# Index weights projected inside the padded rotary key matrix, and the last 16 value rows on two column strips

## The reference, cut to what matters

```python
proj = u @ w_in                 # u: 528 x 1024
qa, ka, va, qb, ckv, krope, qi, ki, wi, ga, gb = jnp.split(proj, list(np.cumsum(SPLITS)[:-1]), axis=-1)
y_a = stick_breaking(qa, ka, va, pos)                       # uses va: 528 x 512
...
krope = partial_rope(krope[:, :, None, :], pos)[:, :, 0]    # krope: 528 x 16
ki = partial_rope(ki[:, :, None, :], pos)[:, :, 0]          # ki: 528 x 64
# in dsa_attention, for each query:
s_idx = jax.nn.relu(jnp.einsum('bqhd,bkd->bqhk', qi, k_idx))
score = jnp.einsum('bqh,bqhk->bqk', wi, s_idx)              # wi: 528 x 8, one index weight per head
_, sel = lax.top_k(score, topk)
```

## Time and profile before

| | |
|---|---|
| median of 3 runs | 2608.38 us (2603.45 to 2608.44) |
| the profiled execution | 2611.73 us |
| its span in the profile | 2609.8 us |
| TensorE busy, share of the span | 2296.4 us, 88% |
| VectorE busy | 961.0 us, 37% |
| ScalarE busy | 451.7 us, 17% |
| mean granted clock of TensorE | 0.94 |
| DMA over the span | 137 GB/s |

### The profile page before, as it was taken

How to read it: one execution, slowest core, us unless ns; L and a number is a source line. 1 busy time by engine, 2 the same in 40 slices (tenths; PEclk the granted TensorE clock), 3 DMA queues, 4 the chain that set the end, 5 groups by cost and what they waited for, 6 DMA issues and landing times.

```text
span 2609.8 us, 26212 instructions
## 1 busy us (share of the span) xinstructions
PE 2296.4 (88%) x10107; PEld 1560.8 (60%) x10107; DVE 961.0 (37%) x1961; ACT 451.7 (17%) x851; POOL 50.8 (2%) x76
## 2 busy tenths in 40 slices
PE   7999999989989999999989997779999587777783
PEld 5888887336644888887558774456785332222231
DVE  5454433133743455434310207876651300000003
ACT  2000001253351001000210014432113000000001
POOL 0000000000000000000000000000000000000001
PEclk9999999999999999999989987789999699989997
DMA  3232222111005323231132210000332589999996
GB/s 128 65 97 87 87 88 91 46 35 33 1 9 181 118 79 97 75 119 57 41 90 69 65 41 1 1 9 1 97 113 92 226 372 429 428 430 429 429 415 246
DMA packets 172359, 359.92 MB, mean 138 GB/s; under 512 B 15665, under 2 KB 144305, under 8 KB 155874
## 3 DMA queue, kind: packets, MB, share of 16 engines
q1 hardware_dynamic: 163744, 326.89, 33.8%
q0 software_dynamic: 5600, 21.10, 2.1%
q10 hardware_dynamic: 2914, 10.56, 1.0%
HBM read 337.49 MB, written 21.04 MB: 137 GB/s over the span
## 4 chain that ended last, share of the span: by engine, by line
PE 27%; DMA 12%; DVE 5%; issue 4%; DVEq 2%; ACT 1%; POOLq 1%; SPq 1%; POOL 0%; ACTq 0%
DMA M<-w 12%; PE PS L2905 7%; PE PS L69 6%; PE PS L2289 5%; PE PS L2471 2%; PE PS L1563 1%; DVE M L1880 1%; DVEq L1884 1%; PE PS L2044 1%; DVE M L1874 1%; PE PS L1573 1%; PE PS L1986 0%; POOLq L258 0%; DVE M L1896 0%; PE PS L1800 0%
## 5 line engine op out<-in xcount | busy, mean ns | idle before, releaser
L575 PE MATMUL PS<-M 128*128 128x256 f32 x2464 | 542.4, 382 | 12.5 <-DVE M L324 7.3
L575 PEld LDWEIGHTS PS<-M 128*128 128x128 f32 x2464 | 469.2, 191 | 86.6 <-DMA M<-w_ffn_up 13.2
L2905 PE MATMUL PS<-M 128*64 128x512 f32 x1536 | 370.3, 640 | 97.4 <-DMA M<-w 93.1
L2905 PEld LDWEIGHTS PS<-M 128*64 128x64 f32 x1536 | 122.6, 147 | 333.6 <-issue 279.6
L606 PE MATMUL PS<-M 128*128 128x256 f32 x1232 | 268.6, 379 | 4.8 <-DVE M L690 2.5
L606 PEld LDWEIGHTS PS<-M 128*128 128x128 f32 x1232 | 233.4, 190 | 41.7 <-issue 10.3
L69 PE MATMUL PS<-M 128*128 128x264 f32 (+1 forms) x824 | 208.5, 416 | 23.0 <-ACT M L313 9.6
L69 PEld LDWEIGHTS PS<-M 128*128 128x128 f32 x824 | 160.0, 196 | 71.0 <-issue 23.2
L2975 DVE TENSOR_TENSOR M<-M,PS 128x512 f32<-128x512 f32 x16 | 11.0, 687 | 434.3 <-PE PS L2905 434.3
L693 DVE TENSOR_TENSOR M<-M,PS 128x256 f32<-128x256 f32 x220 | 92.6, 421 | 201.1 <-PE PS L575 197.0
L2289 PE MATMUL PS<-M 128*128 128x264 f32 x616 | 142.8, 394 | 8.1 <-DVE M L2388 5.1
(11 more groups left out here) (365 smaller groups left out, 2263.5 us busy)
## 6 DMA issues: line engine op xcount, KB each, us to landing
M<-w SPq DMA_DIRECT2D x64, 2048.0 KB, 21.2
M<-w SPq DMA_DIRECT2D x64, 1024.0 KB, 21.9
M<-w_ffn_gate SPq DMA_DIRECT2D x22, 1024.0 KB, 5.4
M<-w_ffn_up SPq DMA_DIRECT2D x22, 1024.0 KB, 5.4
M<-w_ffn_down SPq DMA_DIRECT2D x16, 1024.0 KB, 5.1
M<-w_in SPq DMA_DIRECT2D x13, 1024.0 KB, 5.3
M<-w_in SPq DMA_DIRECT2D x25, 512.0 KB, 3.8
expert_rows<-M POOLq DMA_DIRECT2D x2, 4096.0 KB, 24.4
```

What stands on the lines that cost most here:

```text
L575: last = nc.tensor.matmul(PS[:, 3 * half + BANK[p], 0:HALF], lhs[:, a, :], rhs[:, a, :], start=p in FIRST and a == 0, stop=p in LAST and a ...
L2905: last = nc.tensor.matmul(PS[ROWS * k:ROWS * k + ROWS, bank, :], wide[:, a * P + ROWS * k:a * P + ROWS * k + ROWS], weights(k), start=star ...
```

## The change

`wi` is no longer a product of its own. Its 8 weight columns are loaded into columns 32 to 39 of KRW, which were zero, so the product that makes the rotary key leaves the index weights, turned, on partitions 32 to 39 of its PSUM banks. ACT copies these 8 rows to a new tile WIT, and the rows 0 to 31 and 64 to 127 to R1; rows 32 to 63 of R1 are set to zero by POOL. Five small jobs then turn WIT back: WIT is stationary (8 partitions, 128 tokens) and an 8 by 8 corner of the identity moves. The last job makes the last 32 tokens on four strips, as before.

The 16-token jobs of `va` are split: columns 0 to 127 of the chunk go to partitions 0 to 15 of the bank, columns 128 to 255 to partitions 32 to 47, in alternate products. ACT copies them out with two instructions.

```diff
-        WIW, WUK, WUV = at(SCR + 6240, KD, 8), at(SCR + 6304, 4 * P), at(SCR + 6816, S1)
+        WUK, WUV = at(SCR + 6304, 4 * P), at(SCR + 6816, S1)
+        WIT = at(SCR + 7536, S2)[0:8]
...
-            sp.dma_start(WIW, w2cols(OFF["wi"], 8)).then_inc(small_in, 16)
+            sp.dma_start(KRW[:, :, 32:40], w2cols(OFF["wi"], 8)).then_inc(small_in, 16)
...
         def proj2_pool(pool):
+            pool.wait_ge(r_out, 2 + 7)
+            nc.gpsimd.memset(R1[32:64, 0, :], 0.0).then_inc(tails_set, 1)
             pool.wait_ge(ck_out, 1)
...
+                    strips = 1 if w == P else 2
                     for a in range(KD):
-                        last = nc.tensor.matmul(PS[0:w, 2 + (k - 1) % 2, 0:256], xnT[:, a, lo:lo + w],
-                                                slot(s, 0, KD, 256)[:, a, :], start=a == 0, stop=a == KD - 1)
+                        for m in range(strips):
+                            cols = slice(m * P, m * P + 256 // strips)
+                            last = nc.tensor.matmul(PS[32 * m:32 * m + w, 2 + (k - 1) % 2, 0:256 // strips],
+                                                    xnT[:, a, lo:lo + w], slot(s, 0, KD, 256)[:, a, cols],
+                                                    start=a == 0, stop=a == KD - 1)
...
             for t in range(5):
                 k = after("pe", v2_free)
                 pe.wait_ge(v2_free, k)
+                if t == 0:
+                    pe.wait_ge(ck_out, 1)
                 for m in range(4 if t == 4 else 1):
                     to, lo, w = (slice(32 * m, 32 * m + 32), TAIL0, 32) if t == 4 else (slice(0, P), t * P, P)
-                    for a in range(KD):
-                        last = nc.tensor.matmul(PS[to, 2 + (k - 1) % 2, 0:8], xnT[:, a, lo:lo + w], WIW[:, a, :],
-                                                start=a == 0, stop=a == KD - 1)
+                    last = nc.tensor.matmul(PS[to, 2 + (k - 1) % 2, 0:8], WIT[:, lo:lo + w], ident[0:8, 0:8], start=True, stop=True)
                 last.then_inc(v2_ready, 1)
-            pe.wait_ge(tails_set, 1)
+            pe.wait_ge(tails_set, 2)
...
-            for k in range(2):
-                act.wait_ge(ck_ready, k + 1)
-                nc.scalar.activation(G2.row(R1[:, k, :]), G2.psum(PS, 2 * k), ACT.Copy).then_inc(r_x, 1)
+            act.wait_ge(ck_ready, 1)
+            nc.scalar.activation(G2.row(WIT), G2.psum(PS, 0, 32, 40), ACT.Copy)
+            nc.scalar.activation(G2.row(R1[0:32, 0, :]), G2.psum(PS, 0, 0, 32), ACT.Copy)
+            act.wait_ge(tails_set, 1)
+            nc.scalar.activation(G2.row(R1[64:P, 0, :]), G2.psum(PS, 0, 64, P), ACT.Copy).then_inc(r_x, 1)
+            act.wait_ge(ck_ready, 2)
+            nc.scalar.activation(G2.row(R1[:, 1, :]), G2.psum(PS, 2), ACT.Copy).then_inc(r_x, 1)
...
+                if w < P and n == 256:
+                    nc.scalar.activation(dest[:, 0:P], PS[0:w, 2 + (k - 1) % 2, 0:P], ACT.Copy)
+                    nc.scalar.activation(dest[:, P:n], PS[32:32 + w, 2 + (k - 1) % 2, 0:P], ACT.Copy).then_inc(v2_free, 1)
+                    continue
```

## The result

| | before | changed |
|---|---|---|
| median of 5 runs | 2608.38 us (2598.64 to 2611.20) | 2587.46 us (2582.75 to 2592.32) |
| ratio, 95% interval | | 0.9932, 0.9907 to 0.9957 |
| the profiled execution | 2611.73 us | 2587.01 us |
| its span | 2609.8 us | 2585.1 us |

The changed kernel is faster by 17.7 us by the ratio (0.7%; 11 to 24 us by its interval), 20.9 us by the medians. Forecast were 18.0 us and 2590.4 us. In a later comparison, six runs of it against eleven of before, the ratio was 0.9944 (0.9927 to 0.9961).

A forecast was written before the change was run, and what follows sets the result against it. PE alone was taken to bound the stage; -12.0, -2.5 and -3.5 us sum to -18.0, giving 2593.7 us by the profiled execution and 2590.4 us from the median; range 2584.8 to 2600.5 us.

The forecast's parts named there:

- `wi` jobs: Index weight products on PE: 14.4 us shrinks to 2.4 us, -12.0 us (bounds -13.0 and -8.6).
- WUV jobs: Products right behind the index weights: 8.25 us becomes 5.75 at full clock, -2.5 us (bounds 0 and -3.1).
- two 16-token jobs: `va` jobs split on two column strips: 1.75 us each instead of 3.5, -3.5 us (bounds +0.7 and -3.5).
- rotary key's split, zeroing, new waits: ACT's extra copies at the rotary key, POOL's zeroing and PE's wait on `ck_out`: all hidden, 0 us.
- the sum, by the stretch: All terms together, -18.0 us; measured from the first `va` product to the first KB product.
- PE alone bounds the place, and the gain reaches the end: PE's products alone form the chain from 1482 to 1568 us; the experts' weight stream shifts earlier as a whole.
- The clock: At the `wi` products PE's clock fell from 1.00 to 0.50 and stayed low, mean 0.68, over the WUV jobs.
- The clock holds behind the short thin row: With only 2.4 us of small products, PE's clock stays full through the WUV jobs, worth -2.5 us.
- rival 2: Thin products still pull the clock down at the WUV jobs: sum about -15 us, 2593.5 us; 0.17 with another rival.
- The strips overlap: In the 16-token `va` jobs, products on two column strips run at once: 1.75 us a job, not 3.5.
- The added work is hidden: ACT's extra rotary key copies have 5 us of cover; POOL's 1.2 us zeroing ends 6 us early; 0 us.
- Slower, by the attention stage's clock: Clock stays low throughout the attention stage behind the changed lines: net +20 us, 2628 us; chance 0.03.

The follow-up runs named there:

- e6: Changed kernel with the five small jobs' outputs in one PSUM bank and one copy of 40 columns; first `va` to first KB product 39.06 us, changed kernel 39.67.
- e3: Kernel before, each of the five `wi` jobs placed behind a `va` job of the second chunk; first `va` to first KB product 50.03 us, before 58.08.
- e2: Changed kernel with the 16-token jobs back on one strip of 256 columns; first `va` to first KB product 42.88 us, ratio to before 0.9928.
- e4: Changed kernel with both halves of a 16-token job on one column strip, in two PSUM banks; 3.60 us a job, first `va` to first KB product 44.61.
- e5: Changed kernel with the 16-token jobs on four column strips of 64 columns, four ACT copies; 1.04 us a job, first `va` to first KB product 39.99.
- e11: The changed kernel with four column strips of 64 columns, profiled a second time; first `va` to first KB product again 39.99 us.
- e7: Changed kernel with each small turn done eight times; turns 12.22 us, WUV jobs 7.07, first `va` to first KB product 51.58.

## Why the prediction was right

Its steps against what was measured, in us:

| step | forecast | measured |
|---|---|---|
| `wi` jobs | -12.0 | 14.38 to 1.77: -12.6 |
| WUV jobs | -2.5 | 8.16 to 5.62: -2.5 |
| two 16-token jobs | -3.5 | 2 x (3.56 to 1.87): -3.4 |
| rotary key's split, zeroing, new waits | 0 | 0: 23.46 before and after |
| the sum, by the stretch | -18.0 | -18.4 |

- **PE alone bounds the place, and the gain reaches the end**: right. The chain has the same members, with one ACT copy of 0.19 us where the prediction looked for a wait on ACT, and the experts' stream moved with it, 563.0 us long for 563.3.
- **The `wi` jobs**: right in kind, 0.6 us too dear. I let two full trips to ACT of 1.16 us stand before the first WUV job; e6 shows that only 0.64 us of the 1.77 are trips.
- **The clock**: I read from the earlier trace rows that the thin products cost their successors time. It was more than the 2.5 us that I booked under the WUV jobs. From e3 to e2 the stretch goes from 50.03 to 42.88 us: taking out 56 products is worth 7.15 us at full clock. The step from before to e3, with no product gone, is worth 8.05 us. The strips are the last 3.2 us, to 39.67. The sum was right since I took the `wi` jobs' 14.4 us from the trace, slow clock included.
- **The clock holds behind the short thin row**: right for this kernel in both of its profiles. But rival 2 was underrated as a mechanism: it came true in e4, e5 and e11, at 1.6 us each, half of its price, since the clock was back before KB. In that the result had some luck. The 2.4 us that rival 2 reads from the earlier trace rows are 2.6 by the mean of the second window (0.61 over 2.72 us).
- **The strips overlap**: right. Measured are 1.87 us a job with two strips, 1.04 with four, and 3.60 on one strip (e4). The rule of the Trainium skill in "TensorE: Matmul & The Clock Gate", Part 3, by which a weight load is hidden only behind products of other row groups, would have had 3.6 us or more a job on two strips, as the prediction read it; the measurement decides against it. The estimate of 2.2 us from the speed-up that the same part of the Trainium skill gives for three strips was too slow too.
- **The added work is hidden**: right. ACT had 5.29 us to spare; the zeroing took 0.53 us, less than my 1.2, and lay 7 us ahead of its use.
- **Slower, by the attention stage's clock**: no run shows it. What follows the stretch took 1042.7 to 1048.9 us in all of them, before 1046.05.

What stays open is when a short thin row pulls the clock down. With 2.12 us of small jobs it fell in both executions; with 1.77, 1.59 and 1.13 us it held, in four profiles; but with 1.65 us behind a job on one strip (e4) it fell. The number of small products doesn't decide it, since e4 and the changed kernel have the same eight. Nor does a fixed time: by the means of the windows the clock fell 2.4 us (e4) to 4.9 us (e7) behind the first small product, and 2.6 in the kernel before. I have no rule for it from these runs, and the changed kernel may lose the 1.6 us in an execution that wasn't profiled.

## What to carry to other kernels

Price a product by its weight load: one that moves 8 columns behind a load of 128 costs 0.21 us, so small outputs belong in the zero columns of a product that is made anyway. Look at the granted clock beside the busy time: a row of thin products can cost as much by slowing itself and the wide ones behind it as by its count, and dealing it out among wide products gave that back here (8.05 us) with no work removed. A narrow output is worth spreading over column strips, as long as the copies that it multiplies don't come before a short job.

## What was not expected of the hardware

- Four column strips run as four: the job's 64 records of 64 columns took 1.04 us, against 1.87 us for 32 of 128 on two strips and 3.60 for the same 32 on one. Each doubling came close to halving.
- The clock can fall after the thin products have ended. By the means of the windows above it fell 0.7 us (e4), 0.8 us (e5) and 0.6 us (e11) into wide products, and it was these that ran at half speed.
- Two profiles of one kernel agree in the stretch to 0.01 us (39.67 and 39.67; 39.99 and 39.99) while their spans differ by 2.5 and 8.7 us. The scatter of the total lies elsewhere, and a gain of 2 us is found in the stretch and lost in the median.
